# A decoder layer's merge stage: order of the gate loads, and two output tiles at its end

## The reference

```
y_pool = (pooled * pool_scale) @ w_branch_pool        # 512 -> 1024
y_att  = o.reshape(b, s, 256) @ w_branch_att          # 256 -> 1024
merged = sigmoid(gate_pool) * y_pool + sigmoid(gate_att) * y_att
y      = merged @ w_out                               # 1024 -> 1024
x      = x + gt_m * rmsnorm(y, g_post_mix)
```

## Time and profile before

| | |
|---|---|
| runs before (3) | 2692.35, 2706.5, 2700.36 us; median 2700.36 us |
| profiled execution | 2698.82 us |
| its span, first to last instruction | 2697.1 us |
| granted clock of TensorE, mean | 0.940 |
| attend | until 1227.8 us of the span |
| merge | 1227.8 to 1418.27 us |
| mix_out | 1418.27 to about 1664.5 us |

### The profile page before, as it was taken

How to read it: one execution, slowest core, us unless ns; L and a number is a source line. 1 busy time by engine, 2 the same in 40 slices (tenths; PEclk the granted TensorE clock), 3 DMA queues, 4 the chain that set the end, 5 groups by cost and what they waited for, 6 DMA issues and landing times. The chain is left out here.

```text
span 2697.1 us, 39079 instructions
## 1 busy us (share of the span) xinstructions
PE 2390.0 (89%) x13485; PEld 2038.7 (76%) x13486; DVE 1346.5 (50%) x1712; ACT 959.0 (36%) x1621; POOL 525.2 (19%) x386
## 2 busy tenths in 40 slices
PE   3599999999999978888879995598999999999990
PEld 3488888877888857776667884588889989999980
DVE  7554323222111137755562445888666385756536
ACT  3200000000111125544332221587666385655633
POOL 2311111111222221000004542221222122212210
PEclk8699999999999989968998997799999999999995
DMA  6114242412364554326775434599999598979857
GB/s 234 47 63 140 95 142 94 141 64 94 132 206 167 195 203 141 118 77 197 234 234 169 149 140 156 173 351 359 315 307 292 149 342 250 289 229 286 253 149 295
DMA packets 312858, 517.14 MB, mean 192 GB/s; under 512 B 23485, under 2 KB 228821, under 8 KB 303448
## 3 DMA queue, kind: packets, MB, share of 16 engines
q1 hardware_dynamic: 281978, 418.81, 45.4%
q0 software_dynamic: 18144, 66.07, 9.6%
q10 hardware_dynamic: 12672, 31.46, 3.1%
HBM read 386.02 MB, written 130.24 MB: 191 GB/s over the span
## 5 line engine op out<-in xcount | busy, mean ns | idle before, releaser
L418 PE MATMUL proj_psum<-h_hi,proj_w_hi 128*128 128x512 f32 x1216 | 481.1, 396 | 19.8 <-POOL proj_w_lo L399 18.7
L419 PE MATMUL proj_psum<-h_lo,proj_w_hi 128*128 128x512 f32 x1216 | 480.7, 395 | 0.0
L420 PE MATMUL proj_psum<-h_hi,proj_w_lo 128*128 128x512 f32 x1216 | 480.6, 395 | 0.0
L453 DVE COPY proj_out<-proj_psum 128x512 f32<-128x512 f32 x152 | 123.5, 814 | 633.5 <-PE proj_psum L420 632.9
L1689 PE MATMUL moe_p_gu<-moe_hi_gu,moe_xT_hi 128*128 128x256 f32 x1536 | 438.2, 285 | 1.7 <-DVE moe_xT_lo L1798 1.7
L1691 PE MATMUL moe_p_gu<-moe_hi_gu,moe_xT_lo 128*128 128x256 f32 x1536 | 429.8, 280 | 0.0
L1690 PE MATMUL moe_p_gu<-moe_lo_gu,moe_xT_hi 128*128 128x256 f32 x1536 | 429.7, 280 | 0.0
L1617 DVE TENSOR_TENSOR moe_lo_gu<-raw_gu,moe_hi_gu 128x1024 fp32r<-128x1024 f32 x256 | 302.8, 1222 | 28.1 <-ACT moe_hi_gu L1611 22.3
L1689 PEld LDWEIGHTS moe_p_gu<-moe_hi_gu,moe_xT_hi 128*128 128x128 f32 x1536 | 290.8, 189 | 4.2 <-issue 2.1
L1690 PEld LDWEIGHTS moe_p_gu<-moe_lo_gu,moe_xT_hi 128*128 128x128 f32 x1536 | 291.7, 190 | 2.1
L1691 PEld LDWEIGHTS moe_p_gu<-moe_hi_gu,moe_xT_lo 128*128 128x128 f32 x1536 | 291.1, 190 | 0.0
(11 more groups left out here) (282 smaller groups left out, 3677.1 us busy)
## 6 DMA issues: line engine op xcount, KB each, us to landing
raw_gu<-in_w_exp_gate SPq DMA_DIRECT2D x256, 256.0 KB
raw_gu<-in_w_exp_up SPq DMA_DIRECT2D x256, 256.0 KB
raw_d<-in_w_exp_down SPq DMA_DIRECT2D x128, 512.0 KB
projected<-proj_out SPq DMA_DIRECT2D x38, 1024.0 KB, 4.3
proj_raw<-in_w_in SPq DMA_DIRECT2D x38, 512.0 KB, 10.9
att_qkv<-projected SPq DMA_DIRECT2D x18, 1024.0 KB
proj_w_rest<-in_w_ada SPq DMA_DIRECT2D x8, 2048.0 KB
y_sum<-proj_w_rest SPq DMA_DIRECT2D x20, 512.0 KB, 8.3
```

The lines of the kernel that those rows point to most:

```text
L418: pe.matmul(bank, w_hi[:, u, k, :], h_hi[:, k, tok], start=(k == 0), stop=False)
L419: pe.matmul(bank, w_hi[:, u, k, :], h_lo[:, k, tok], start=False, stop=False)
L420: mm = pe.matmul(bank, w_lo[:, u, k, :], h_hi[:, k, tok], start=False, stop=(k == KD - 1))
L453: ins = dve.tensor_copy(view[:, ds(tg * per, per), :], psum[:, u, tg, :].rearrange("p (m r) -> p m r", r=dilation))
```

## The change

- In merge the attention gates get 5 slots instead of 4 (RA). SP's round n now loads attention gate n + 4 first, and behind it pooled gate n + 12, whose slot was stored in round n - 2. The 14 pooled slots stay; before the loop one pooled gate fewer and one attention gate more is loaded.
- `y`, the 4 banks of the output product, is allocated before merge and passed to both stages. Merge's small products and transposes use its banks; merge's own psum has 4 banks.
- At the end of merge TensorE multiplies output tiles 0 and 1: weight rows 0 to 4 for both, then rows 5 to 7, each with a semaphore of its own (`late_loaded`). mix_out starts with tile 2; TensorE counts `y_half` up by 4 at once.
- The router's weights and biases are loaded in attend, behind the pooled input, and kept. mix_out's waits for them go.
- SP's order at the start of mix_out is x tile 0, modulation, merged tile 2, merged tile 3, x tile 1.

```diff
-    RP, RA, BANKS = 14, 4, 4
+    RP, RA, BANKS = 14, 5, 4
...
+                sp.dma_start(wr[:, :, 0:EG], w_group_router[0].rearrange("(k p) e -> p k e", p=P)).then_inc(next_loaded, 16)
+                sp.dma_start(wr[:, :, EG:NR], w_expert_router[0].rearrange("(k p) e -> p k e", p=P)).then_inc(next_loaded, 16)
+                sp.dma_start(rbias[:, 0:EG], b_group_router[0:1, :].partition_broadcast(P)).then_inc(next_loaded, 16)
+                sp.dma_start(rbias[:, EG:NR], b_expert_router[0:1, :].partition_broadcast(P)).then_inc(next_loaded, 16)
...
-        z_bank = lambda n: psum[:, n % 2, :]
-        o_bank = lambda p: psum[:, 2 + p % 2, :].rearrange("p (k c) -> p k c", k=KA)
-        y_bank = lambda turn: psum[:, 4 + turn % BANKS, :]
+        z_bank = lambda n: y[:, 0, ds((n % 2) * 512, 512)]
+        o_bank = lambda p: y[:, 1, ds((p % 2) * 512, 512)].rearrange("p (k c) -> p k c", k=KA)
+        y_bank = lambda turn: psum[:, turn % BANKS, :]
...
-                for n in range(6, RP - 1):
+                for n in range(6, RP - 2):
                     load_p(n)
...
-                    if n + RP - 1 < UNITS:
-                        load_p(n + RP - 1)
                     if n + RA - 1 < UNITS:
                         load_a(n + RA - 1)
+                    if n + RP - 2 < UNITS:
+                        load_p(n + RP - 2)
...
-                        pool.dma_start(w[:, k - EARLY_K, :], out_cut[i, ds(k * P, P), :]).then_inc(out_loaded, 16)
+                        pool.dma_start(w[:, k - EARLY_K, :], out_cut[i, ds(k * P, P), :]).then_inc(late_loaded[k - EARLY_K], 16)
...
+                pe.wait_ge(m_lo_ready, AHEAD)
+                pe.wait_ge(out_loaded, 32 * EARLY_K)
+                for ks in (range(EARLY_K), range(EARLY_K, KD)):
+                    for t in range(AHEAD):
+                        for half in range(2):
+                            cols = ds(half * 512, 512)
+                            for k in ks:
+                                if k >= EARLY_K:
+                                    pe.wait_ge(late_loaded[k - EARLY_K], 32)
+                                out_tile(pe, y[:, t, cols], z_hi, z_lo, t, wo_hi, wo_lo, w_hi, w_lo, k, cols)
...
-                load_merged(2)
-                sp.dma_start(mod[:, :, :].rearrange("p m d -> p (m d)"), mod_dram[0:1, :].partition_broadcast(P)).then_inc(mod_loaded, 16)
-                load_x(0)
+                load_x(0)
+                sp.dma_start(mod[:, :, :].rearrange("p m d -> p (m d)"), mod_dram[0:1, :].partition_broadcast(P)).then_inc(mod_loaded, 16)
+                load_merged(2)
                 load_merged(3)
                 load_x(1)
...
-                product(0, 0)
-                product(0, 1)
-                pe.wait_ge(small_loaded, 64)
+                pe.sem_inc(y_half, 4)
                 for t in range(TILES + 2):
-                    if t + 1 < TILES:
+                    if 1 <= t < TILES - 1:
                         product(t + 1, 0)
```

More of the change, by code:

```diff
@@ L25 @@
 SUM_TILES = 20
+NR = EG + NE
 ADA_PAIR, ROW_PAIR, CUT_PAIR, ZERO_PAIR = 2, 11, 12, 14
@@ L525, with attend @@
 MASKED = 1e38
-def attend(nc, proj, ident, att, branch_cut, w_pool_group, pool_scale, wb_hi, wb_lo, wg, scale, pooled):
+def attend(nc, proj, ident, att, branch_cut, w_pool_group, pool_scale, wb_hi, wb_lo, wg, scale, pooled,
+           w_group_router, w_expert_router, b_group_router, b_expert_router, wr, rbias):
     units = []
@@ L630, in _ @@
                     sp.wait_ge(stored[i], 16 * len(range(i, N, 4)))
-                sp.wait_ge(next_loaded, 16 * 3)
+                sp.wait_ge(next_loaded, 16 * 7)
                 sp.wait_ge(branch_loaded, 16 * 2 * KP_MIX)
@@ L804, in merged_tile, with out_tile, merge @@
     return z[:, t // 2 % 2, ds(2 * (t % 2), 2), :].rearrange("p g (k c) -> p (g k) c", c=P)
-def merge(nc, proj, att, ident, w_hi, w_lo, wg, scale, pooled, z_hi, z_lo, out_cut, wo_hi, wo_lo, merged):
+def out_tile(pe, bank, z_hi, z_lo, t, wo_hi, wo_lo, late_hi, late_lo, k, cols):
+    m_hi, m_lo = merged_tile(z_hi, t)[:, k, :], merged_tile(z_lo, t)[:, k, :]
+    w_hi, w_lo = (wo_hi[:, k, cols], wo_lo[:, k, cols]) if k < EARLY_K else (late_hi[:, k - EARLY_K, cols], late_lo[:, k - EARLY_K, cols])
+    pe.matmul(bank, m_hi, w_hi, start=(k == 0), stop=False)
+    pe.matmul(bank, m_hi, w_lo, start=False, stop=False)
+    return pe.matmul(bank, m_lo, w_hi, start=False, stop=(k == KD - 1))
+def merge(nc, proj, att, ident, w_hi, w_lo, wg, scale, pooled, z_hi, z_lo, out_cut, wo_hi, wo_lo, merged, y):
     CHUNK = 512
@@ L826, in merge @@
         gate_a = s.sb("gate_a", [P, RA, CHUNK])
-        psum = s.ps("psum", [P, 8, 512])
+        psum = s.ps("psum", [P, 4, 512])
         pooled_loaded = [s.sem(f"pooled_loaded{g}") for g in range(KP)]
@@ L833, in merge @@
         mT_loaded = [s.sem(f"mT_loaded{i}") for i in range(AHEAD)]
+        late_loaded = [s.sem(f"late_loaded{k}") for k in range(EARLY_K, KD)]
         (z_summed, z_hi_ready, z_lo_ready, steps, shifted, coef_exp, o_ready, o_turned, o_hi_ready, o_lo_ready, p_gated, a_gated,
@@ L922, in _ @@
                     sp.wait_ge(m_stored[i], 16 * len(range(i, UNITS, RP)))
-                sp.wait_ge(out_loaded, 32 * KD)
+                sp.wait_ge(out_loaded, 32 * EARLY_K)
             @block.gpsimd
@@ L952, in turn @@
                         for i in range(2):
[L953 removed]
+                            tr = pe.transpose(y[:, 1, ds((p % 2) * 512 + (2 * k + i) * P, P)], o[:, p % 2, i, ds(k * P, P)], ident[:, :])
                     tr.then_inc(o_turned, 1)
@@ L1107, in _, with mix_out @@
                         apply_p(n + KD)
-NR = EG + NE
-def mix_out(nc, x, merged, pooled, z_hi, z_lo, wo_hi, wo_lo, late_hi, late_lo, mod_dram, ident, w_group_router, w_expert_router,
-            b_group_router, b_expert_router, x1_dram, h_dram, logits):
+def mix_out(nc, x, merged, pooled, z_hi, z_lo, wo_hi, wo_lo, late_hi, late_lo, y, mod_dram, ident, wr, rbias, x1_dram, h_dram, logits):
     with ExitStack() as ctx:
@@ L1238, in product @@
                     cols = ds(half * 512, 512)
-                    m_hi, m_lo = merged_tile(z_hi, t), merged_tile(z_lo, t)
-                    if half == 0 and t >= 2:
+                    if half == 0:
                         pe.wait_ge(m_lo_ready, t - 1)
@@ L1243, in product @@
                     for k in range(KD):
[L1244 to L1248, removed]
+                        mm = out_tile(pe, bank, z_hi, z_lo, t, wo_hi, wo_lo, late_hi, late_lo, k, cols)
                     mm.then_inc(y_half, 1)
@@ L1948, in build @@
             pooled = mid("pooled", [P, POOL_TILES, 512])
-            attend(nc, proj, ident, att, branch_cut, w_pool_group, pool_scale, wb_hi, wb_lo, wg, scale, pooled)
+            wr, rbias = mid("wr", [P, KD, NR]), mid("rbias", [P, NR])
+            attend(nc, proj, ident, att, branch_cut, w_pool_group, pool_scale, wb_hi, wb_lo, wg, scale, pooled,
+                   w_group_router, w_expert_router, b_group_router, b_expert_router, wr, rbias)
+            y = mixed.enter_context(nc.psum_tensor("y", [P, 2, D], F32))
             wo_hi, wo_lo = mid("wo_hi", [P, EARLY_K, D], F32R, "right"), mid("wo_lo", [P, EARLY_K, D], F32R, "right")
             z_hi, z_lo = mid("z_hi", [P, 2, POOL_TILES, 512], F32R, "right"), mid("z_lo", [P, 2, POOL_TILES, 512], F32R, "right")
-            merge(nc, proj, att, ident, wb_hi, wb_lo, wg, scale, pooled, z_hi, z_lo, out_cut, wo_hi, wo_lo, merged)
-            mix_out(nc, x, merged, pooled, z_hi, z_lo, wo_hi, wo_lo, wb_hi, wb_lo, mod_dram, ident, w_group_router, w_expert_router,
-                    b_group_router, b_expert_router, x1_dram, h_dram, logits)
+            merge(nc, proj, att, ident, wb_hi, wb_lo, wg, scale, pooled, z_hi, z_lo, out_cut, wo_hi, wo_lo, merged, y)
+            mix_out(nc, x, merged, pooled, z_hi, z_lo, wo_hi, wo_lo, wb_hi, wb_lo, y, mod_dram, ident, wr, rbias, x1_dram, h_dram, logits)
         raw_gu, raw_d = top("raw_gu", [P, GU, 2, 2, H2]), top("raw_d", [P, KE, D])
```

12 lines of the change are left out of this document (2 added, 10 removed).

## The result

| | before | after |
|---|---|---|
| median of 9 runs each | 2696.52 us | 2674.7 us |
| lowest to highest | 2688.77 to 2706.5 | 2670.14 to 2688.98 |
| profiled execution, span | 2697.1 us | 2674.9 us |
| ratio of the runs, 95% interval | | 0.9927, 0.9906 to 0.9947 |

The change makes the kernel 21.8 us faster by the medians.

A forecast was written before the change was run, and what follows sets the result against it. It took TensorE to be bound by late attention gates behind SP's store waits. Tile 2 starting 19.0 us earlier, clock +2.4, gave -16.6 from 2698.8, so 2682.2; plus 1.5 for the median, 2683.7 us, range 2677 to 2696.

The forecast's parts named there:

- I take 18.5: Merge: time recovered by the new gate order and slots, 18.5 us, between ends of 9 and 20.2.
- part 1: Merge, gate order and slots: attention gates leave earlier without the store wait, recovering 18.5 us.
- the full stretch of 36.2 us: Merge's first 36.2 us, TensorE never idle: taken to show nothing else holds it when gates are in time.
- The tail's 2.3 us: Merge's last attention products: the stall for unit 27's gate would go, giving 2.3 us.
- +1.9 us, a loss: Merge's end and output stage: moving output tiles 0 and 1 by itself costs 1.9 us.
- the 18.8: Output stage's start: tile 2 starts 18.8 us after the stage begins, after merged tile 3, split, root and product.
- the clock's 2.4: Output tile 2: TensorE's clock falls after the idle time, costing 2.4 us, ends 1.5 and 3.
- cost 0, at most 3: Attention: the router loads moved there cost 0, at most 3 us if they hold the first stores back.
- A: Rival, merge: gates are held by bandwidth, not queue order; slower than before, 2702.3 us if nothing is recovered; chance 0.10.
- B: Rival, merge: stores and loads stretch each other, only 9 us recovered, 2693 us; chance 0.17.
- C: Rival, output stage's start: shorter chain and all 20.2 us back, 2679 us; chance within the forecast's 0.73.
- D: Rival, attention: router loads delay it by 3 us, 2687 us; chance within the forecast's 0.73.

The follow-up runs named there:

- 1: Kernel before with only the changed kernel's gate loads (5 attention slots, attention gate first, pooled gate n+12): 2673.48 us, ratio 0.9901.
- 3: Kernel before with only the new load order (attention gate first, pooled gate n+12), still 4 attention slots: 2675.79 us, ratio 0.9904.
- 9: Kernel before, pooled gate still first but that of round n+12, so its store is a round old; 4 slots: 2673.43 us, ratio 0.9909.
- 10: Kernel before with attention gate first, pooled gate n+13 still waiting for the newest store, 4 slots: 2682.19 us, ratio 0.9944.
- 4: Changed kernel with the gate loads of the kernel before: 2706.28 us, ratio to before 1.0024.
- 6: Changed kernel with the four router loads back at the output stage's start, behind x tile 1: 2673.94 us, ratio to before 0.9906.

## Why the prediction was right and wrong

**The mechanism held.** The SP queue's wait for the newest store makes its rounds too long (6.6 us, and 4.6 without it), and the merge waits for its gates; without that wait every late gate that held TensorE goes, and the late turns of its transposes with it (experiments 1, 3 and 9). What the prediction did not see is that putting the attention gate ahead of the wait recovers 16.9 of the 21.0 us even with the wait kept (10). The products moved to the merge's end bring nothing by themselves (1 and 4), and the output stage then waits for its chain from merged tile 3, 17.6 us long.

**The term that was mis-sized: "I take 18.5".** Measured 22.3 us, more than the stated upper end of 20.2. Two errors, both in part 1. First, the allowance of 1.7 us for stalls that stay: none stayed, and the full stretch of 36.2 us had said so. Second, the sum of idle time and clock (12.7 + 5.2 = 17.9 us) for the stretch up to 1393.3, which shortened by 129.1 - 109.3 = 19.8 us. Busy time is no good base here: a matmul is drawn 0.39 us long while the next starts 0.233 us after it, so a stall of up to 0.16 us behind it counts as busy. Where a 512-column matmul is followed later than its 0.233 us, such hidden stalls add up to 4.1 us in this stretch before and 1.1 after, so 3.0 us were missing in the sum. Against that, the 5.2 us for the clock was too much, for it was taken over the whole stretch, the 12.7 us of idle time included: with 12.7 of idle time and 3.0 hidden, 4.1 of the 19.8 us are left for it. Counting instructions would have been better: 24 x 18 x 0.233 = 100.7 us of products, and the small products and transposes on top, which in the full stretch can be read from the timeline; the result 109.3 us leaves 8.6 for them. The tail's 2.3 us was right (13.4 us between the last pooled and the last attention matmul before, 1393.13 to 1406.57, and 11.0 after, 1377.6 to 1388.59).

**The moved products: "+1.9 us, a loss".** Measured -2.0 + 2.1 = +0.1 us, which is no different from nothing. Of the terms, 22.4 was 22.24, the barrier's 1.2 was 1.24 (1410.84 to 1412.08), the 18.8 was 17.6, because merged tile 3 landed 12.2 us and not 13.5 after the stage's start, and the clock's 2.4 was 2.1. The 3.7 + 1.6 us from split to tile was 1429.73 - 1424.32 = 5.4.

**The router loads, "cost 0, at most 3".** Probably too low: the runs taken together point to some 4.7 us (experiments 4 and 6), though none shows it by itself. The 7.3 us of issues became 11.3 (993.6 to 1004.9 in the changed kernel's SP queue), so that the first result left at 1004.93 instead of 1003.02, or 0.8 us later counted from the attention's first load (977.22 and 976.11). The slack of 10 us all but covered them, so the cost, if it is real, does not come from this delay alone.

**The base.** The forecast subtracted from the median of three runs, 2700.36 us; the nine runs of before give 2696.52. That is 3.8 of the 9.0 us by which the forecast is high; the change itself was 21.8 us against 16.7. Neither alone would have put the time outside the range. Merge and output stage gave 22.2 us in the profiles and the whole 21.8 by medians; kernels without the early router loads gained 2.6 us more on the whole than in these stages (see 6), so part of this agreement is luck.

**The rivals.** A would need gates still late at a high DMA share: the share did rise to 0.82, exactly as worked out, and TensorE still never waited for a gate. B, half back, fell with it. C had the right direction, all back and a shorter chain, at 2679, and was given too little room below. D, the router loads, was set aside for its 10 us of slack, and the runs now speak for it more than against it.

**The page's rule.** By the figures of "DMA: Bandwidth & Descriptors" of the Trainium skill, section "Anatomy of one DMA", a store would take an estimate of 2.6 us. From that the prediction drew that the queue order would hardly matter. The page gives the figures for single transfers issued by GpSimd, and these stores are issued by SP beside other traffic. They took 2.1 us at the least, 5.0 at the median and 11.6 at the most before the change, so the measurement decides; and the order alone was worth 21 us in the merge (3 and 9).

## What to carry to other kernels

Where one queue both sends results out and reloads their slots, let no load wait for the store just sent: the wait makes each round at least as long as a store's landing and its issues. If it has to stay, send the more urgent loads ahead of it, which was worth 16.9 of 21.0 us here; a further slot for the loads behind it gave 4.2. Look at the waits of the DMA queue itself, not only at those of the engines; and price the recovery by counting instructions at their full pace. Work moved ahead of a barrier gains only if what the next stage must do first is moved with it: the products alone gave 0, with the splits of the next tiles 11 to 12 us. And that the issues of a small load fit a gap of the queue does not show that moving it there is free: compare whole kernels with it and without it, with many runs.

## What was not expected of the hardware

The 256 KB stores landed no faster when the queue was relieved: the merge's 32 stores took 5.0 us at the median in both kernels, and the first 18, those that the pooled gates waited for, 5.6 us in the mean against 4.9, at a share of 0.82 instead of 0.70; attention gates took 5.9 at the median against 4.9. The relief came from waiting for older stores, not from quicker ones. And the attention, whose computing is the same in all kernels, took from 247.6 to 265.0 us in fourteen profiles, with TensorE's clock between 0.80 and 0.98 in the same 70 us stretch: more than most of what this study measures. Without the early router loads it was 247.6 to 254.6 us, in nine profiles.
